# Block transposes on VectorE and SBUF transfers in place of TensorE transposes in the second block's attention

## The chip, the cores and the metric

The kernel runs on one core of a Trainium2 chip. The metric is device microseconds from start to end of one execution; the kernel before takes 1913.06 us (median of three runs, 1912.67 to 1913.16). Everything is float32; most matrix products run as three products of rounded parts (high by high, high by low, low by high), in the type fp32r.

## The reference, cut to what matters

Two blocks follow each other on a sequence of 512 positions with model width 2048. Only the second is touched: a projection to eight streams, eight heads of "stick-breaking" attention (A), eight heads of chunk-band attention (B), a gate, and an output projection.

```
h = rms_norm(x, norm_g)
qa, ka, va, ga, qb, kb, vb, gb = split(h @ w_in)
# A: w[t,s] = exp(log_sigmoid(z) + sum of log_sigmoid(-z) over s<j<t), s < t
ya = einsum('bhts,bhsd->bhtd', w, va)
# B: q, k normed per head, bias by distance, band of 9 chunks of 64
yb = einsum('bhcip,bhcpd->bhcid', softmax(scores + bias), vband)
x  = x + concat(ya * silu(ga), yb * silu(gb)) @ w_out
```

## The kernel before

Activations lie transposed: channels on the 128 partitions, the 512 positions along the row. A "unit" is one tile of 128 output channels of a projection: 16 contraction tiles `k`, three matmuls of 512 columns each, 48 matmuls in one PSUM bank (`gemm`). Head `h` of the second block has eight units `u + j` with `u = U_D2 + 8h`: qa, ka, va, ga, qb, kb, vb, gb. The weights of a unit come by one 1 MB transfer that SyncE (SP) issues, as soon as the unit two before it has been split; ScalarE copies its high part (`hi`), VectorE subtracts for its low part (`lo`), for unit `u + j + 2` behind unit `u + j`.

TensorE's own order is written out by hand in `d2_head`. Between tiles of the units it puts the attention of the same head: scores A (unit 3, after two tiles), scores B (unit 6, before its last two tiles), the value products A (unit 5, after two tiles) and B (after unit 7). Weights and probabilities come out of the scores with queries on the partitions, and the product needs keys there; values come with channels on the partitions and need positions there. So TensorE transposes: four 128x128 blocks of the values and ten of the weights, for A and again for B, 28 in a head. They go to PSUM (`pb`), from where ScalarE and VectorE make high and low parts (`VTH`, `VTL`; `WBH`, `WBL`; `PTH`, `PTL`). Each engine has its list, and semaphores join them; whatever stands behind a waiting instruction on its engine waits too. Heads 0 to 6 are a loop, head 7 is written out; in it the splitting of the output projection's operands (`operand_hi`, `operand_lo`) stands between the steps of B. Lines: 1480 is any matmul, 1483 a transpose, 398 and 829 the splitting of weights, 422 and 838 that of operands, 245 the weight transfer.

Of the kernel before, what the change touches and what calls it, by code (L numbers as in the profile page):

```python
# [12 lines left out]
P = 128  # L13
S = 512
D = 2048
KT = D // P
NB = S // P
# [26 lines left out]
TURN_AT = 11  # L44
# [42 lines left out]
def build(nc, w, w_ab, xT, memT, rows_in, consts, negatives, params, ws_t, bs_b, ln_rows, rel, x1_dram, rows_dram, outT):  # L87
    with ExitStack() as ctx:
# [61 lines left out]
        VTH, VTL = vtok_t[:, 0:S], vtok_t[:, S:2 * S]  # L150
        WBH, WBL, PTH, PTL = w_hi_t[:, 0:n], w_lo_t[:, 0:n], parts[:, 0:n], parts[:, n:2 * n]
# [61 lines left out]
        def v3(a):  # L213
# [3 lines left out]
        UP = [0, 512, 896, 1152]  # L217
        UN = [S - P * b for b in range(NB)]
# [4 lines left out]
            mem_in1 mem_in2 mem_in3 mem_in4 next_in m_ps wab_in wab ab_mm ab_sb row_sq diag x_ps x_r  # L223
            mixed
            dve_steps act_steps 
            ab_ps ab_exp ab_act ab_g ab_cum ab_e ab_gc
# [7 lines left out]
            a_vps a_vtok a_hi a_lo a_z a_l a_x a_w a_tp a_wh a_wl a_o  # L234
            g_y g_sig b_sq b_sql b_hi b_lo b_ss b_r b_n b_vps b_vh b_vtok b_bias b_sc b_add b_max b_exp b_p b_tp b_pt b_ptl b_o 
# [7 lines left out]
        def _(sp):  # L243
# [27 lines left out]
            with sp.Fori(1, U_END // 2 - 1) as i:  # L271
                for slot in range(2):

                    sp.wait_ge(sem["hi"], 8 * i + 4 * slot + 4)
                    sp.wait_ge(sem["lo"], 8 * i + 4 * slot + 4)
                    load(2 * i + 2 + slot, slot)
# [111 lines left out]
        def _(act):  # L388
# [115 lines left out]
            act.wait_ge(sem["ab_exp"], 1)  # L504
# [5 lines left out]
            act.wait_ge(sem["ab_gc"], 1)  # L510
            A(gate["egl"][:, :], gate["a"][:, :], ACT.Exp)
            A(gate["ekd"][:, :], gate["t"][:, :], ACT.Exp).then_inc(sem["ab_e"], 1)
# [229 lines left out]
            def d2_head(h, last=False):  # L742
                u = 8 * h + U_D2

                def next_hi(j):
                    hi(u + j + 2, (U_D2 + j) % 2)

# [18 lines left out]
                for b in range(NB):  # L766
                    act.wait_ge(sem["a_tp"], NB * h + b + 1)
                    A(WBH[:, UP[b]:UP[b] + UN[b]], pb[b][:, 0:UN[b]], ACT.Copy).then_inc(sem["a_wh"], 1)

                for j in range(2):  # L770
                    act.wait_ge(sem["evac"], u + (5 + j))
                    A(SQ[0:H, :], Y[0:H, :], ACT.Square)
                    A(E[0:H, :], Y[H:P, :], ACT.Square).then_inc(sem["b_sq"], 1)
                    next_hi(4 + j)

                    rsqrt(E, pb[5][:, :], -1.0 / P, "b_ss", 2 * h + j + 1, "b_r")
                    act.wait_ge(sem["b_n"], 2 * h + j + 1)
                    A([QH, KH][j], [QB, KBN][j], ACT.Copy).then_inc(sem["b_hi"], 1)
# [5 lines left out]
                act.wait_ge(sem["b_vps"], h + 1)  # L784
                A(VTH, pb[4][:, :], ACT.Copy).then_inc(sem["b_vh"], 1)
# [4 lines left out]
                for b in range(NB):  # L790
                    act.wait_ge(sem["b_tp"], NB * h + b + 1)
                    A(PTH[:, UP[b]:UP[b] + UN[b]], pb[b][:, 0:UN[b]], ACT.Copy).then_inc(sem["b_pt"], 1)
                if last:
                    act.wait_ge(sem["mixed"], M1 + 2 * DN - 1)
# [11 lines left out]
            with act.Fori(0, DN - 1) as h:  # L806
                st.enter(h, 2 * NB + 2 + 2 + 2)
                d2_head(h)
                st.leave(DN - 1)
            d2_head(DN - 1, True)  # L810
# [9 lines left out]
        def _(dve):  # L820
# [56 lines left out]
            V.tensor_tensor(ab, ab, par[:, C_LN:C_LN + KT].rearrange("p (k j) -> p k j", j=1).broadcast_to([P, KT, AB]), ALU.mult)                .then_inc(sem["wab"], 1)  # L877
# [17 lines left out]
            dve.wait_ge(sem["ab_mm"], 1)  # L895
            dve.wait_ge(sem["x_r"], 1)
            V.tensor_tensor(pair(SS, 0), pair(pb[0][:, :], 0), pair(XR, 0), ALU.mult)
            V.tensor_tensor(pair(SS, 1), turned(pb[0][:, :]), turned(XR), ALU.mult).then_inc(sem["ab_sb"], 1)
            lo(U_V + 3, 1)
            dve.wait_ge(sem["ab_ps"], 1)  # L900
# [7 lines left out]
            V.tensor_tensor(gv["t"], gv["a"], gv["g"], ALU.max).then_inc(sem["ab_exp"], 1)  # L908
# [4 lines left out]
            V.scalar_tensor_tensor(gv["g"], gv["a"], -1.0, a8, ALU.mult, ALU.mult).then_inc(sem["ab_g"], 1)  # L913
# [3 lines left out]
            dve.wait_ge(sem["ab_cum"], 1)  # L917
# [3 lines left out]
            V.tensor_tensor(gate["t"][:, :], gate["a"][:, :], gate["gc"][:, :], ALU.subtract).then_inc(sem["ab_gc"], 1)  # L921
            dve.wait_ge(sem["ab_e"], 1)
# [404 lines left out]
            def d2_head(h, last=False):  # L1327
# [17 lines left out]

                for j, dst in enumerate((QA, KA, VA)):
                    unit(u + j)
                    V.scalar_tensor_tensor(dst, bank[slot(j)][:, :], SCALE if j == 0 else 1.0, R12, ALU.mult, ALU.mult)\  # L1348
                        .then_inc(sem["evac"], 1)
                    next_lo(j)  # L1350
# [3 lines left out]
                dve.wait_ge(sem["a_vps"], h + 1)  # L1354
                st.then(V.tensor_copy(VTH, pb[4][:, :]))
                V.tensor_tensor(VTL, pb[4][:, :], VTH.bitcast(F32), ALU.subtract).then_inc(sem["a_vtok"], 1)
# [13 lines left out]
                for b in range(NB):  # L1370
                    t = slice(UP[b], UP[b] + UN[b])
                    dve.wait_ge(sem["a_wh"], NB * h + b + 1)
                    V.tensor_tensor(WBL[:, t], pb[b][:, 0:UN[b]], WBH[:, t].bitcast(F32), ALU.subtract).then_inc(sem["a_wl"], 1)
                gate_silu(2 * h + 1, SGA)
                for j in range(2):
# [5 lines left out]
                    V.tensor_tensor(SQH[H:P, :], SQ[0:H, :], FOLD.bitcast(F32), ALU.subtract).then_inc(sem["b_sql"], 1)  # L1381
                    next_lo(4 + j)
                    if j == 0:
# [22 lines left out]
                V.tensor_tensor(VBT, bank[slot(6)][:, :], R12, ALU.mult).then_inc(sem["evac"], 1)  # L1406
                next_lo(6)
                for c in range(NB):
# [3 lines left out]
                    V.tensor_scalar(pc, pc, small[:, 4 + c:5 + c], None, ALU.mult).then_inc(sem["b_p"], 1)  # L1412
                dve.wait_ge(sem["b_vh"], h + 1)
                V.tensor_tensor(VTL, pb[4][:, :], VTH.bitcast(F32), ALU.subtract).then_inc(sem["b_vtok"], 1)
# [3 lines left out]
                for b in range(NB):  # L1418
                    t = slice(UP[b], UP[b] + UN[b])
                    dve.wait_ge(sem["b_pt"], NB * h + b + 1)  # L1420
                    V.tensor_tensor(PTL[:, t], pb[b][:, 0:UN[b]], PTH[:, t].bitcast(F32), ALU.subtract).then_inc(sem["b_ptl"], 1)
                if last:
# [6 lines left out]
                gate_silu(2 * h + 2, SGB)  # L1429
                dve.wait_ge(sem["b_o"], h + 1)  # L1430
                out = (h + DN) * S
                out = big[:, bass.ds(out, S)] if not isinstance(out, int) else big[:, out:out + S]
                V.tensor_tensor(out, pb[4][:, :], SGB, ALU.mult).then_inc(sem["mixed"], 1)
                dve.wait_ge(sem["mixed"], 2 * h + (M1 + 2))
                if last:
# [8 lines left out]
            with dve.Fori(0, DN - 1) as h:  # L1444
                st.enter(h, 1 + 4 * NB + 1 + 1 + NB + 2 + 2)
                d2_head(h)
                st.leave(DN - 1)
            d2_head(DN - 1, True)
# [29 lines left out]
        def _(pe):  # L1478
# [79 lines left out]
            def ab_gemm():  # L1558

                pe.wait_ge(sem["wab"], 1)  # L1560
# [7 lines left out]
                ins.then_inc(sem["ab_mm"], 1)  # L1568
# [17 lines left out]
            pe.wait_ge(sem["ab_sb"], 1)  # L1586
            for c in range(NB):
                ins = tp(pb[0][:, c * P:(c + 1) * P], blk(SS, c))
            ins.then_inc(sem["ab_ps"], 1)
# [3 lines left out]
            pe.wait_ge(sem["ab_g"], 1)  # L1593
# [4 lines left out]
            mm(pb[0][:, n:2 * n], C["ones"], gate["g"][:, :]).then_inc(sem["ab_cum"], 1)  # L1598
# [218 lines left out]
            def d2_head(h):  # L1817
# [11 lines left out]
                def values(hi_part, low_part):  # L1829

                    for b in range(NB):
                        t, out = slice(UP[b], UP[b] + UN[b]), pb[4][:, b * P:S]
# [5 lines left out]
                d2(1)  # L1838
                d2(2)
                d2(3, 0, 2)  # L1840
                pe.wait_ge(sem["evac"], u + 3)
                for c in range(NB):
                    ins = tp(pb[4][:, c * P:(c + 1) * P], blk(VA, c))
                ins.then_inc(sem["a_vps"], 1)

# [4 lines left out]
                d2(4, 0, TURN_AT)  # L1850

                pe.wait_ge(sem["a_w"], NB * h + NB)
                for b in range(NB):
                    for c in range(b, NB):
                        ins = tp(pb[b][:, (c - b) * P:(c - b + 1) * P], WB[:, DO[c] + b * P:DO[c] + (b + 1) * P])
                    ins.then_inc(sem["a_tp"], 1)
                d2(4, TURN_AT)
                d2(5, 0, 2)
                pe.wait_ge(sem["a_wl"], NB * h + NB)
                pe.wait_ge(sem["a_vtok"], h + 1)  # L1860
                values(WBH, WBL).then_inc(sem["a_o"], 1)
                for j in range(2):
                    d2(5 + j, 0 if j else 2, 8)
                    pe.wait_ge(sem["b_sql"], 2 * h + j + 1)
                    mm(pb[5][:, :], sums[:, P:2 * P], SQH).then_inc(sem["b_ss"], 1)
                    d2(5 + j, 8, 14)
                    if j == 1:
# [114 lines left out]
```

## Time and profile before

| | |
|---|---|
| median of the runs | 1913.06 us |
| profiled execution, span from first to last instruction | 1910.9 us |
| outside that span, against the median | 2.2 us |
| TensorE busy | 1903.4 us, 100% of the span |
| VectorE, ScalarE, GpSimd busy | 61%, 43%, 6% |
| one head of the second block, from gate to gate | 98.2 us |

The profile gives the profiled execution's span; its own time outside the span is not listed apart, and the 2.2 us above is the difference to the median. A busy share of a matmul engine counts instructions that overlap, so it only says that something was in flight; the rate is read from starts, or from the chain of waits, whose pieces follow each other without overlap.

### The profile page before, as it was taken

How to read it: one execution, taken by the hardware profiler on the slowest of the kernel's cores; microseconds unless marked ns; L12 is line 12 of the kernel's file. 1: busy time of each engine (PE TensorE's matmuls, PEld its weight loads, DVE VectorE, ACT ScalarE, POOL GpSimd, SP SyncE). 2: the span in 40 equal slices, each digit the busy share in tenths (PEclk: the TensorE clock that was granted, in tenths of full speed). 3: DMA queues.
4: the chain of work that ended last, by engine and by line, in shares of the span. 5: the costliest groups of instructions: out<-in, count | busy, mean ns of one | idle time of the engine just before them, and what ended most of it. 6: DMA issues, size and time to landing. Idle time of an engine off the chain costs nothing.

```text
span 1910.9 us, 27480 instructions
## 1 busy us (share of the span) xinstructions
PE 1903.4 (100%) x9126; PEld 1586.7 (83%) x9126; DVE 1172.9 (61%) x2193; ACT 817.9 (43%) x1603; POOL 112.1 (6%) x172
## 2 busy tenths in 40 slices
PE   9999999999999999999999999999999999999999
PEld 7788888888888888888888888888888888888887
DVE  6565687778877775634556565656564646466333
ACT  5653444544445434423444343434343434344211
POOL 0100011001111010001000000000000000000010
PEclk9999999999999999999999999999999999999999
DMA  8722232223232223344332222222222222223341
GB/s 323 297 89 88 78 99 78 71 71 99 77 77 77 69 73 112 123 152 143 121 116 72 91 90 88 93 88 93 88 89 92 71 102 79 88 88 121 137 160 66
DMA packets 33817, 202.09 MB, mean 106 GB/s; under 512 B 4592, under 2 KB 4720, under 8 KB 13296
## 3 DMA queue, kind: packets, MB, share of 16 engines
q1 hardware_dynamic: 23904, 165.95, 24.2%
q0 software_dynamic: 9728, 35.49, 6.8%
q8 instruction: 26, 0.43, 0.1%
q10 hardware_dynamic: 144, 0.10, 0.0%
q14 instruction: 15, 0.12, 0.0%
HBM read 193.10 MB, written 8.42 MB: 105 GB/s over the span
## 4 chain that ended last, share of the span: by engine, by line
PE 95%; DVE 2%; DMA 1%; ACT 1%; issue 0%; SPq 0%; DVEq 0%; ACTq 0%
PE gemm L1480 82%; PE pb L1480 12%; PE pb L1483 2%; DMA raw<-in_w 1%; DVE w_lo L829 1%; DVE act_lo L838 0%; DMA scratch<-in_memT 0%; ACT w_hi L398 0%; DVE scratch L1039 0%; ACT act_lo L435 0%; DVE parts L849 0%; DVE scratch L937 0%; ACT scratch L406 0%; ACT scratch L407 0%; ACT scratch L405 0%
## 5 line engine op out<-in xcount | busy, mean ns | idle before, releaser
L1480 PE MATMUL gemm<-act_hi,w_hi 128*128 128x512 f32 x2304 | 921.0, 400 | 0.2 <-DVE act_lo L838 0.2
L1480 PE MATMUL gemm<-act_lo,w_hi 128*128 128x512 f32 x2320 | 902.8, 389 | 0.1
L1480 PE MATMUL gemm<-act_hi,w_lo 128*128 128x512 f32 x2304 | 899.8, 391 | 0.0
L398 ACT ACTIVATE w_hi<-raw 128x512 fp32r<-128x512 f32 x616 | 337.3, 619 | 406.7 <-PE gemm L1480 385.9
L1480 PEld LDWEIGHTS gemm<-act_hi,w_lo 128*128 128x128 f32 x2304 | 432.4, 188 | 93.3
L1480 PEld LDWEIGHTS gemm<-act_lo,w_hi 128*128 128x128 f32 x2320 | 436.7, 188 | 83.4 <-ACT w_hi L398 0.4
L1480 PEld LDWEIGHTS gemm<-act_hi,w_hi 128*128 128x128 f32 x2304 | 433.4, 188 | 82.2 <-issue 0.8
L829 DVE TENSOR_TENSOR w_lo<-raw,w_hi 128x512 fp32r<-128x512 f32 x624 | 400.1, 696 | 144.7 <-ACT w_hi L398 137.2
L1480 PEld LDWEIGHTS pb<-scratch 128*128 128x128 f32 x932 | 136.0, 192 | 26.3 <-DVE scratch L1200 5.9
L1480 PE MATMUL pb<-scratch 128*128 128x128 f32 (+3 forms) x932 | 141.4, 279 | 2.2 <-DVE scratch L844 1.7
L1348 DVE SCALAR_TENSOR_TENSOR scratch<-gemm,scratch 128x512 f32<-128x512 f32 x24 | 16.6, 692 | 150.1 <-PE gemm L1480 149.9
L405 ACT ACTIVATE scratch<-scratch 128x512 f32<-128x512 f32 x56 | 35.2, 628 | 87.0 <-DVE scratch L1040 43.7
L338 POOL TENSOR_TENSOR scratch<-scratch,cst 128x256 f32<-128x256 f32 x56 | 47.4, 853 | 416.3 <-DVE scratch L1091 243.4
L417 ACT ACTIVATE scratch<-pb,eps 128x512 f32<-128x512 f32 x41 | 28.3, 690 | 97.8 <-PE pb L1480 97.8
L1039 DVE SCALAR_TENSOR_TENSOR scratch<-scratch,par 128x511 f32<-128x511 f32 (+2 forms) x72 | 54.0, 750 | 9.8 <-DVE scratch L1037 2.5
L713 ACT ACTIVATE scratch<-big 128x512 f32 (+1 forms) x16 | 10.1, 632 | 108.7 <-DVE big L1287 108.7
L1287 DVE TENSOR_TENSOR big<-gemm,scratch 128x512 f32 (+1 forms) x16 | 11.0, 687 | 69.1 <-PE gemm L1480 69.1
L594 ACT ACTIVATE scratch<-pb 128x128 f32<-128x128 f32 x40 | 11.1, 278 | 91.3 <-PE pb L1480 90.9
L1483 PEld LDWEIGHTS pb<-cst,scratch 128*128 128x128 f32 x364 | 42.9, 140 | 7.1 <-DVE scratch L999 0.3
L1483 PE MATMUL pb<-cst,scratch 128*128 128x128 f32 x364 | 48.5, 272 | 0.0
L371 POOL DMA_DIRECT2D scratch<-in_rel x7 | 3.8, 538 | 657.6 <-DVE scratch L1402 657.6
L406 ACT ACTIVATE scratch<-scratch 128x512 f32<-128x512 f32 x56 | 35.4, 632 | 1.8
(296 smaller groups left out, 1614.8 us busy)
## 6 DMA issues: line engine op xcount, KB each, us to landing
raw<-in_w SPq DMA_DIRECT2D x154, 1024.0 KB, 4.8
scratch<-in_rows_in POOLq DMA_DIRECT2D x6, 1024.0 KB, 8.5
big<-in_xT POOLq DMA_DIRECT2D x4, 1024.0 KB, 11.4
scratch<-rows POOLq DMA_DIRECT2D x16, 256.0 KB, 6.5
scratch<-in_xT POOLq DMA_DIRECT2D x16, 256.0 KB, 2.9
x<-big POOLq DMA_DIRECT2D x16, 256.0 KB, 2.3
scratch<-x POOLq DMA_DIRECT2D x16, 256.0 KB, 4.0
outT<-scratch POOLq DMA_DIRECT2D x15, 256.0 KB, 3.8
```

Of the source, the lines that this page charges most:

```text
L338: nc.gpsimd.tensor_tensor(v3(blk(ML, NB * (k % 2), 2)), pair(AT, 0), C[f"level{k}"].rearrange("p (c t) -> p c t", c=1).broadcast_to([P, 2, ...
L398: A(w_hi[slot][:, c], raw[slot][:, c], ACT.Copy).then_inc(sem["hi"], 1)
L405: st.then(A(E, SS, ACT.Exp, scale=-1.0))
L406: st.then(A(E, E, ACT.Ln, bias=1.0))
L417: st.then(A(dst, src, ACT.Ln, bias=eps[:, 0:1], scale=scale))
L594: A(UI[:, 0:P], pb[2][:, 0:P], ACT.Copy).then_inc(sem["u_sb"], 1)
L829: V.tensor_tensor(w_lo[slot][:, c], raw[slot][:, c], w_hi[slot][:, c].bitcast(F32), ALU.subtract)\
L1039: st.then(V.scalar_tensor_tensor(Y[:, 3 - k:], SS[:, :S - 3 + k], tap(k), Y[:, 3 - k:], ALU.mult, ALU.add))
L1287: V.tensor_tensor(x1, bank[u0 % 2][:, :], blk(XIN, NB * j, NB), ALU.add).then_inc(sem["evac"], 1)
L1348: V.scalar_tensor_tensor(dst, bank[slot(j)][:, :], SCALE if j == 0 else 1.0, R12, ALU.mult, ALU.mult)\
L1480: return nc.tensor.matmul(out, a, b, start=start, stop=stop, skip_group_check=skip)
L1483: return nc.tensor.transpose(out, a, C["ident"])
```

## The change

In heads 0 to 6 no TensorE transpose is left; in head 7 only the ten of the probabilities B stay. VectorE transposes each 32x32 block within its rows' quadrant (`turn_values`, `turn_weights`) into `VTURN` or `SPB`, and SP issues 16 transfers (`regroup`) that move, for each pair of partition quadrants, 32 rows from the one into the other, into `VRAW` or `WB`. A row of one transfer has 512 bytes for values and 1280 for weights. ScalarE then copies the high part and VectorE subtracts the low part, both reading in one order and writing in another (`by_row`, `in_order`). The value products move: A from tile 2 to tile 12 of unit 5, B from the end of its head to tile 2 of the next head's unit 1 (in head 7 it stays behind unit 7). B's gate and its product with the output follow into the next head. Head 0 is written out as well, so the loop has heads 1 to 6. SP's list for the second block is written out, with waits for the turns between the weight loads. The renamed semaphores of the first block (`ab_*`) change no order.

```diff
+            def regroup(dst, src, size, done):
+                n = size * Q
+                for a in range(NB):
+                    for q in range(NB):
+                        sp.dma_start(dst[q * Q:(q + 1) * Q, a * n:(a + 1) * n], src[a * Q:(a + 1) * Q, q * n:(q + 1) * n])\
+                            .then_inc(sem[done], 16)
+            for h in range(DN):
+                u = U_D2 + 8 * h + 4
+                one_load(u)
+                one_load(u + 1)
+                sp.wait_ge(sem["v_turn"], 2 * h + 1)
+                regroup(VRAW, VTURN, NB, "va_in")
+                one_load(u + 2)
+                one_load(u + 3)
+                sp.wait_ge(sem["w_turn"], 2 * h + 1)
+                regroup(WB, SPB, SLOTS, "aw_in")
+                one_load(u + 4)
+                one_load(u + 5)
+                sp.wait_ge(sem["v_turn"], 2 * h + 2)
+                regroup(VRAW, VTURN, NB, "vb_in")
+                one_load(u + 6)
+                if h < DN - 1:
+                    sp.wait_ge(sem["w_turn"], 2 * h + 2)
+                    regroup(WB, SPB, SLOTS, "bp_in")
+                one_load(u + 7)
...
+            def value_hi(ready, n):
+                act.wait_ge(sem[ready], n)
+                A(in_order(VTH, NB), by_row(VRAW, NB), ACT.Copy).then_inc(sem["v_hi"], 1)
+            def weight_hi(ready, n):
+                act.wait_ge(sem[ready], n)
+                for s in (slice(0, SLOTS // 2), slice(SLOTS // 2, SLOTS)):
+                    A(in_order(WBH, SLOTS)[:, s], by_row(WB, SLOTS)[:, s], ACT.Copy).then_inc(sem["a_wh"], 1)
...
+                if tail:
+                    weight_hi("bp_in", 256 * h)
                 for j in range(3):
                     next_hi(j)
...
-                for b in range(NB):
-                    act.wait_ge(sem["a_tp"], NB * h + b + 1)
-                    A(WBH[:, UP[b]:UP[b] + UN[b]], pb[b][:, 0:UN[b]], ACT.Copy).then_inc(sem["a_wh"], 1)
+                value_hi("va_in", 256 * h + 256)
                 for j in range(2):
                     act.wait_ge(sem["evac"], u + (5 + j))
                     A(SQ[0:H, :], Y[0:H, :], ACT.Square)
                     A(E[0:H, :], Y[H:P, :], ACT.Square).then_inc(sem["b_sq"], 1)
+                    if j == 0:
+                        weight_hi("aw_in", 256 * h + 256)
                     next_hi(4 + j)
...
                 next_hi(6)
-                act.wait_ge(sem["b_vps"], h + 1)
-                A(VTH, pb[4][:, :], ACT.Copy).then_inc(sem["b_vh"], 1)
+                value_hi("vb_in", 256 * h + 256)
...
+            def turn_values(src):
+                V.transpose(by_row(VTURN, NB), src).then_inc(sem["v_turn"], 1)
+            def turn_weights(src, c):
+                n = min(c + 1, NB - 1)
+                ins = V.transpose(by_row(SPB, SLOTS)[:, c:c + 3 * n - 2:3], src[:, DO[c]:DO[c] + n * P])
+                if c == NB - 1:
+                    ins = V.transpose(by_row(SPB, SLOTS)[:, 7:8], src[:, DO[c] + n * P:DO[c] + DNN[c]])
+                return ins
...
+                if tail:
+                    gate_silu(2 * h, SGB)
+                    weight_lo(4 * h - 2)
...
+                for i, c in enumerate(reversed(range(NB))):
+                    dve.wait_ge(sem["a_w"], NB * h + i + 1)
+                    ins = turn_weights(WB, c)
+                ins.then_inc(sem["w_turn"], 1)
                 gate_silu(2 * h + 1, SGA)
+                value_lo(2 * h + 1, "a_vtok")
...
-                d2(1)
+                d2(1, 0, 2)
+                if tail:
+                    pe.wait_ge(sem["mixed"], 2 * h + (M1 - 1))
+                    pe.wait_ge(sem["b_vtok"], h)
+                    pe.wait_ge(sem["a_wl"], 4 * h)
+                    values(WBH, WBL, UT).then_inc(sem["b_o"], 1)
+                d2(1, 2)
```

## Rows read from the trace of the kernel before

**Rows 1.** The page: busy times, granted clock in 40 slices, and the chain's engines.

```profile
PE 1903.4 (100%) x9126; PEld 1586.7 (83%) x9126; DVE 1172.9 (61%) x2193; ACT 817.9 (43%) x1603; POOL 112.1 (6%) x172
...
PEclk9999999999999999999999999999999999999999
...
PE 95%; DVE 2%; DMA 1%; ACT 1%; issue 0%; SPq 0%; DVEq 0%; ACTq 0%
```

**Rows 2.** Busy time by stretch: stretch, length, busy (instructions) by engine, clock, DMA.

```profile
1289.40:1387.60 98.20, 98.20 (x462) 82.25 (x461) 57.11 (x108) 41.06 (x84) 0.54 (x1) 1.00 0.25 88
```

**Rows 3.** Chain of waits through that head: start, us, what, count.

```profile
1295.81 1.09 PE pb L1483 x10
1296.90 4.81 PE gemm L1480 x21
...
1303.57 4.14 PE gemm L1480 x18
...
1307.94 10.88 PE gemm L1480 x48
...
1329.03 0.44 PE pb L1483 x4
1329.47 4.13 PE gemm L1480 x18
1333.60 1.09 PE pb L1483 x10
1334.69 4.11 PE gemm L1480 x18
1338.80 1.85 PE pb L1480 x12
...
1374.73 0.44 PE pb L1483 x4
```

**Rows 4.** All transposes: duration min/median/max in ns, first and last start.

```profile
L1483 PE MATMUL pb<-cst,scratch x364: 270/272/328, 60.8 to 1727.3; 128*128 128x128 f32 x182
```

**Rows 5.** VectorE in order of time: start, us, instruction, idle before it.

```profile
1290.47 2.49 DVE L829 TENSOR_TENSOR w_lo<-raw,w_hi 128x512 fp32r<-128x512 f32 x4
...
1300.46 0.69 DVE L1377 TENSOR_TENSOR scratch<-gemm,scratch 128x512 f32<-128x512 f32 x1 [1.26 <-PE gemm L1480]
...
1327.14 0.68 DVE L1406 TENSOR_TENSOR scratch<-gemm,scratch 128x512 f32<-128x512 f32 x1
...
1332.62 0.49 DVE L1412 TENSOR_SCALAR scratch<-scratch,small 128x512 f32<-128x512 f32 x1
...
1338.84 0.69 DVE L1338 TENSOR_TENSOR scratch<-gemm,scratch 128x512 f32<-128x512 f32 x1 [2.45 <-PE gemm L1480]
...
1351.64 0.69 DVE L1348 SCALAR_TENSOR_TENSOR scratch<-gemm,scratch 128x512 f32<-128x512 f32 x1 [5.43 <-PE gemm L1480]
```

**Rows 6.** ScalarE in order of time: the four exponentials that finish weights A.

```profile
1290.53 1.53 ACT L764 ACTIVATE scratch<-scratch 128x512 f32<-128x512 f32 x4
```

**Rows 7.** The first block's block transposes on VectorE, durations in ns.

```profile
L1188 DVE STREAM_TRANSPOSE scratch<-scratch x40: 431/438/441, 258.1 to 696.4; 128x256 f32<-128x256 f32 x40
```

**Rows 8.** SP's issue instructions: duration min/median/max in ns, first and last start.

```profile
L245 SPq DMA_DIRECT2D raw<-in_w x154: 327/333/343, 11.1 to 1867.6; - x154
...
L249 SPq DMA_DIRECT2D raw<-in_w x6: 403/468/707, 1.0 to 5.2; - x6
```

**Rows 9.** DMA issues: KB each, median us from issue to landing.

```profile
outT<-scratch SPq DMA_DIRECT2D x1, 256.0 KB, 2.0
```

**Rows 10.** Head 7's end: VectorE, ScalarE (order of time), TensorE (chain).

```profile
1719.99 0.68 DVE L1406 TENSOR_TENSOR scratch<-gemm,scratch 128x512 f32<-128x512 f32 x1
...
1726.93 1.43 ACT L792 ACTIVATE parts<-pb 128x512 fp32r<-128x512 f32 x4 [1.36 <-PE pb L1483]
1728.21 4.29 ACT L422 ACTIVATE act_hi<-big 128x512 fp32r<-128x512 f32 x8
...
1733.51 174.16 PE gemm L1480 x768
```

More of the change, by code:

```diff
@@ L270, in _, with loads, one_load @@
                     mem(12, 4, "mem_in4")
[L271 to L276, printed above, removed]
+            def loads(first, past):
+                with sp.Fori(first // 2 - 1, past // 2 - 1) as i:
+                    for slot in range(2):
+                        sp.wait_ge(sem["hi"], 8 * i + 4 * slot + 4)
+                        sp.wait_ge(sem["lo"], 8 * i + 4 * slot + 4)
+                        load(2 * i + 2 + slot, slot)
+            def one_load(u):
+                sp.wait_ge(sem["hi"], 4 * (u - 1))
+                sp.wait_ge(sem["lo"], 4 * (u - 1))
+                load(u, u % 2)
+            def regroup(dst, src, size, done):
[4 more added lines that the diff above has]
+                            .then_inc(sem[done], 16)
+            loads(4, U_D2 + 4)
+            for h in range(DN):
[17 more added lines that the diff above has]
+                one_load(u + 7)
+            loads(U_O2 + 4, U_END)
             sp.wait_ge(sem["evac"], U_O2 + KT)
@@ L804, in d2_head @@
                 next_hi(7)
-            with act.Fori(0, DN - 1) as h:
-                st.enter(h, 2 * NB + 2 + 2 + 2)
+            d2_head(0, False)
+            with act.Fori(1, DN - 1) as h:
+                st.enter(h - 1, 2 * NB + 2 + 2 + 2)
                 d2_head(h)
-                st.leave(DN - 1)
-            d2_head(DN - 1, True)
+                st.leave(DN - 2)
+            d2_head(DN - 1, True, True)
             act.wait_ge(sem["mixed"], M1 + 2 * DN)
@@ L1353, in d2_head @@
                         V.tensor_tensor([QL, KL][j], dst, [QH, KH][j].bitcast(F32), ALU.subtract).then_inc(sem["a_lo"], 1)
-                dve.wait_ge(sem["a_vps"], h + 1)
-                st.then(V.tensor_copy(VTH, pb[4][:, :]))
-                V.tensor_tensor(VTL, pb[4][:, :], VTH.bitcast(F32), ALU.subtract).then_inc(sem["a_vtok"], 1)
+                    if j == 0 and tail:
+                        dve.wait_ge(sem["b_o"], h)
+                        out = (h + (DN - 1)) * S
+                        out = big[:, bass.ds(out, S)] if not isinstance(out, int) else big[:, out:out + S]
+                        V.tensor_tensor(out, pb[4][:, :], SGB, ALU.mult).then_inc(sem["mixed"], 1)
+                        dve.wait_ge(sem["mixed"], 2 * h + M1)
                 for i, c in enumerate(reversed(range(NB))):
@@ L1411, in d2_head @@
                     st.then(V.reciprocal(small[:, 4 + c:5 + c], small[:, 4 + c:5 + c]))
-                    V.tensor_scalar(pc, pc, small[:, 4 + c:5 + c], None, ALU.mult).then_inc(sem["b_p"], 1)
-                dve.wait_ge(sem["b_vh"], h + 1)
-                V.tensor_tensor(VTL, pb[4][:, :], VTH.bitcast(F32), ALU.subtract).then_inc(sem["b_vtok"], 1)
+                    if last:
+                        V.tensor_scalar(pc, pc, small[:, 4 + c:5 + c], None, ALU.mult).then_inc(sem["b_p"], 1)
+                    else:
+                        st.then(V.tensor_scalar(pc, pc, small[:, 4 + c:5 + c], None, ALU.mult))
+                        ins = turn_weights(PB, c)
+                if not last:
+                    ins.then_inc(sem["w_turn"], 1)
+                value_lo(2 * h + 2, "b_vtok")
                 if last:
@@ L1417, in d2_head @@
                         operand_lo(k, 4 * KT)
[L1418 to L1422, printed above, removed]
+                    for b in range(NB):
+                        t = slice(UP[b], UP[b] + UN[b])
+                        dve.wait_ge(sem["b_pt"], b + 1)
+                        V.tensor_tensor(PTL[:, t], pb[b][:, 0:UN[b]], PTH[:, t].bitcast(F32), ALU.subtract).then_inc(sem["b_ptl"], 1)
                     for k in range(4, 8):
@@ L1428, in d2_head @@
                         operand_lo(k, 4 * KT)
[L1429 to L1435, printed above, removed]
+                    gate_silu(2 * h + 2, SGB)
+                    dve.wait_ge(sem["b_o"], h + 1)
+                    V.tensor_tensor(big[:, (h + DN) * S:(h + DN + 1) * S], pb[4][:, :], SGB, ALU.mult).then_inc(sem["mixed"], 1)
+                    dve.wait_ge(sem["mixed"], 2 * h + (M1 + 2))
                     for k in range(12, KT - 1):
@@ L1442, in d2_head @@
                     next_lo(7)
[L1444 to L1445 removed]
+            d2_head(0, False)
+            with dve.Fori(1, DN - 1) as h:
+                st.enter(h - 1, 4 * NB + 1 + 1 + 2 * NB + 2 + 2)
                 d2_head(h)
[L1447 to L1448 removed]
+                st.leave(DN - 2)
+            d2_head(DN - 1, True, True)
             def out_tile(i, j, more=True):
@@ L1814, in _, with d2_head @@
             gemm(U_D2, U_D2 % 2, 12, KT, before=3 * KT)
-            def d2_head(h):
+            def d2_head(h, tail=True, last=False):
                 u = 8 * h + U_D2
@@ L1827, in scores, with values @@
                     return mm3(pb[c][:, 0:DNN[c]], (QH, QL), (KH, KL), c, slice(0, DNN[c]))
-                def values(hi_part, low_part):
+                def values(hi_part, low_part, at):
                     for b in range(NB):
-                        t, out = slice(UP[b], UP[b] + UN[b]), pb[4][:, b * P:S]
+                        t, out = slice(at[b], at[b] + UN[b]), pb[4][:, b * P:S]
                         mm(out, blk(VTH, b), hi_part[:, t], b == 0, False, skip=True)
@@ L1849, in d2_head @@
                 d2(3, 2)
[L1850 to L1861, printed above, removed]
+                d2(4)
                 for j in range(2):
-                    d2(5 + j, 0 if j else 2, 8)
+                    d2(5 + j, 0, 8)
                     pe.wait_ge(sem["b_sql"], 2 * h + j + 1)
                     mm(pb[5][:, :], sums[:, P:2 * P], SQH).then_inc(sem["b_ss"], 1)
-                    d2(5 + j, 8, 14)
-                    if j == 1:
+                    if j == 0:
+                        d2(5, 8, VALUES_AT)
+                        pe.wait_ge(sem["mixed"], 2 * h + M1)
+                        pe.wait_ge(sem["a_vtok"], h + 1)
+                        pe.wait_ge(sem["a_wl"], 4 * h + 2)
+                        values(WBH, WBL, UT).then_inc(sem["a_o"], 1)
+                        d2(5, VALUES_AT)
+                    else:
+                        d2(6, 8, 14)
                         pe.wait_ge(sem["b_lo"], 2 * h + 2)
@@ L1870, in d2_head @@
                             scores(c, QB, KBN).then_inc(sem["b_sc"], 1)
-                    d2(5 + j, 14)
-                d2(7, 0, 4)
-                pe.wait_ge(sem["evac"], u + 7)
-                pe.wait_ge(sem["mixed"], 2 * h + (M1 + 1))
-                for c in range(NB):
-                    ins = tp(pb[4][:, c * P:(c + 1) * P], blk(VBT, c))
-                ins.then_inc(sem["b_vps"], 1)
-                d2(7, 4, 10)
-                pe.wait_ge(sem["b_p"], NB * h + NB)
+                        d2(6, 14)
+                if not last:
+                    d2(7)
+                    return
+                d2(7, 0, 10)
+                pe.wait_ge(sem["b_p"], NB)
                 for b in range(NB):
```

101 lines of the change are left out of this document (60 added, 41 removed).

## The prediction

> **What bounds the kernel now.** I read the page first. TensorE is busy 100% of the span, the chain that ended last lies on it for 95%, and the granted clock is at its full step in every slice [rows 1], which is the 2.4 GHz level. The busy share alone would prove little, since matmuls overlap. So I took one head of the second block: in 98.20 us no idle time of TensorE, VectorE busy 57.11 and ScalarE 41.06 [rows 2]. The chain of waits through this head is TensorE alone, and its pieces add without overlap [rows 3]. A whole unit of 48 matmuls takes 10.88 us there, 0.2267 us a matmul. The bound is therefore the list of TensorE's instructions: what is taken from it shortens the time one for one, as long as no other engine becomes late.
>
> **What is removed.** In a head the chain holds 10 transposes at 1.09 us twice and 4 at 0.44 us twice, 3.06 us [rows 3]. The matmuls after them run a little long too: 21 in 4.81 against 21 x 0.2267 = 4.76, 18 in 4.13 and 18 in 4.11 against 4.08. That adds 0.05 + 0.05 + 0.03 = 0.13 (the value product has such a tail too, 18 in 4.14; it stays). Some of it may be a change of data type that the scores bring anyway, so a head gives 3.06 to 3.19; I take 3.13. Seven heads give 21.9. Head 7 keeps ten, and gives 0.44 + 0.44 + 1.09 + 0.1 = 2.1. Together **24.0 us** (23.4 to 24.4). The matmul instructions that stay keep their number; only their place changes, which costs nothing while TensorE does not wait.
>
> The row of all transposes shows 272 ns each [rows 4], yet ten together advance the chain by 1.09 us, 109 ns each, as the next starts while the last drains. The Trainium skill ("TensorE: Matmul & The Clock Gate", Part 4) gives about 275 ns for a transpose in a kernel; the duration agrees. By that price the 214 transposes would be worth 58.9 us and the time would be 1854. I go by the chain, because only it adds up to the span.
>
> **What VectorE and ScalarE get.** Per head VectorE turns values twice and weights twice. A block transpose of 256 columns takes 438 ns [rows 7]; with about 1 ns a column (a 512-column operation beside it takes 690, by [rows 5]), 512 columns take 0.7 and the five pieces of the weights about 1.9 us in sequence. That is 5.2 us a head, less one copy of 0.7: VectorE goes from 57 to about 62 of 95 us. ScalarE gets 0.6 more. Neither becomes the bound; what counts is when each result is there.
>
> **The new chain A: turn, 16 transfers, high part, low part, product.** In the old clock of the head in [rows 3, 5, 6]: the exponentials end at 1292.06 and VectorE's low part of the weights at 1292.96. Turns to 1294.9, SP starts at 1295.0. Let s be SP's time for one issue. The trace has no row of 16 issues of 32 rows. The nearest are the weight loads, issued singly, 0.333, and the pieces at the kernel's start, issued back to back, median 0.468 and up to 0.707 [rows 8]; the latter ran with other transfers still queued. Between them I take s = 0.43, and keep 0.33 and 0.7 as ends. The last transfer lands 2.0 us after its issue, as the 256 KB store does [rows 9]: 1295.0 + 15 x 0.43 + 2.0 = 1303.5. ScalarE's two copies of 640 columns and VectorE's two subtractions need 2.5 us more: 1306.0. TensorE arrives at tile 12 of unit 5 so: unit 5 begins 15 matmuls into the 21 behind the ten transposes, 1296.90 + 15 x 0.229 = 1300.3 [rows 3], less 1.14 for those transposes, plus twelve tiles of 0.68 and 0.23 for the sum, 1307.5; an instruction starts some 0.1 before its piece of the chain, 1307.4. Slack 1.4 us; it is gone at s = 0.52. Behind ScalarE's wait stand the high parts for unit 6, due five microseconds later, so this wait itself costs nothing.
>
> **Chain B.** The values leave PSUM at 1327.8 [rows 5], are turned at 1328.6, and 16 issues end at 1335.5. The probabilities were ready at 1333.1 [rows 5]; with 0.7 for the values' turn, 1.9 for their own and some waits, 1336.1. SP issues one weight load (0.33) and then 16 more: landed at 1336.2 + 6.45 + 2.0 = 1344.7, low parts at 1347.1. The product stands at tile 2 of the unit that followed the evacuation at 1351.64; 1.6 of transposes less, 0.35 that TensorE is ahead of that row, 1.36 of two tiles: 1351.0. Slack 3.9 us, gone at about s = 0.57.
>
> **SP's own list.** The load of unit 6 would have been issued 3.2 us behind unit 2; now it waits for the values' 16 issues, until about 8.5 us behind it, and lands in 4.8. It is split only behind unit 4, more than 20 us after unit 2. The other loads lose less. Cost: none; without this cover a late load would hold ScalarE, VectorE and TensorE in turn. GpSimd's queue is not touched.
>
> The Trainium skill ("DMA: Bandwidth & Descriptors", Rules for kernel authors) speaks against this change: transfers under 64 KB are mostly overhead, some 2 us each, and should be made one. These have 16 and 40 KB. By that rule the time would be rival 5's. The pieces at the kernel's start speak against that: they were issued about every half microsecond [rows 8], less than any landing time there [rows 9], so none waited for the one before to land.
>
> **Head 7's end.** Here there is no later unit to hide in. Values B leave PSUM at 1720.7 [rows 10], turned 1721.5, landed at 1721.7 + 15 x 0.43 + 2.0 = 1730.2; before, ScalarE had its copy at 1722.9. Behind the wait on ScalarE stand four operand copies and the copies of the probabilities. After the landing come 0.6 for the values, 2.2 for four operands (eight take 4.29) and 1.43 for the probabilities [rows 10], and VectorE's subtractions chase them; the last low part is there 5.2 us after the landing, at 1735.4. TensorE was ready when the projection's piece began less the product before it (1.85 [rows 3]), 1733.51 - 1.85 = 1731.6, now 0.5 earlier for the transposes gone, 1731.1. It stands **4.3 us** (3 at s = 0.33, 8 at 0.7). The operands after it keep some slack: the last one is due 10.2 us into the projection's first unit and comes about 1 us before.
>
> **Sum.** -24.0 + 4.3 = -19.7. On the profiled span, 1910.9 - 19.7 = 1891.2; with the 2.2 us that the median has outside that span, **1893.4 us**.
>
> **Rivals.**
> 1. *A small stall in every head* (s between 0.52 and 0.6, slower landing beside the 1 MB load, or longer turns with scattered output). At s = 0.6 A misses by 1.1 and B by 1.1: 8.8 + 7.7, and the end 6.9, so 1912.5; with A alone missing by half a microsecond, 1898. For it: A has only 1.4 us. Against: the single issues of 0.333. Time 1897 to 1911.
> 2. *SP's issue is the price, and it is slower than before.* One mechanism: 64 issues a head in one in-order list. It decides from s = 0.6 on. At 0.65 A misses by 1.8 us in eight heads and B by 2.7 in seven, 15 + 19, and the end costs 7.6: 1913 - 24 + 42 = 1931. For it: the row reaching 0.707. Against: those issues carried 128 rows and stood behind a full queue.
> 3. *The end hides its wait*: head 7 costs at most 1 us, 1890. For: the trace shows ScalarE idle there in places [rows 10]. Against: the order of ScalarE's list.
> 4. *A transpose costs its duration*: 214 x 0.272 [rows 4] less the end's 4.3, 1859. Against it, the pieces of the chain, which leave no room for it.
> 5. *The transfers run one after another*: 16 x 2.0 [rows 9] = 32 us for each regrouping instead of 8.5, over 20 us late in each of 15 products, above 2200. It is what the skill's rule on small transfers would make of them. Against it, the issues at the start.
>
> **Chances.** Forecast 0.60, rival 1 0.18, rival 2 0.08, rival 3 0.10, rivals 4 and 5 0.02 each. The range reaches from rival 3 into rival 1: 1889 to 1903. No change means within 0.2% (3.8 us), about what a measurement of this kernel can tell: it needs s near 0.6, chance 0.03 out of rival 1. Slower 0.10 (rivals 2 and 5), faster 0.87.
>
> **What would show it.** A head's period of 95.1 us in the chain, with no idle time of TensorE before either value product. SP's 16 issues every 0.43 us, about 6.9 us from first to last; landing about 2 us behind issue. One idle time of TensorE of about 4.3 us before the value product of head 7, put down to VectorE's last low part. The forecast fails if the heads show idle time before the products (rival 1 or 2, told apart by the issue rows), or if the span falls by more than 24.4.

## The result and the profile after: slower by 1.9%

The changed kernel takes 1949.69 us (median of 4, 1948.9 to 1950.7) beside 1913.11 for the kernel before: ratio 1.0194, 95% interval 1.0181 to 1.0206. The forecast was 1893.4, in a range of 1889 to 1903. Its span is 1948.3 us.

The page of the changed kernel first: busy time, share and instructions of each engine, and the chain's shares by engine.

```profile
PE 1898.6 (97%) x8912; PEld 1575.4 (81%) x8912; DVE 1201.2 (62%) x2246; ACT 818.8 (42%) x1581; POOL 112.2 (6%) x172
...
PE 70%; SPq 11%; DVE 11%; DMA 3%; ACT 3%; issue 2%; DVEq 0%; ACTq 0%
```

The 214 matmul instructions are gone (9126 before [rows 1]), but the chain that ended last, 95% TensorE before, now passes through SP's queue for 11% and VectorE for 11%. TensorE's waits say where (engine and line that waited, releaser: us in total, times, longest):

```profile
PE pb L1579 <- DVE w_lo_t L1406: 34.4, 15, 4.1
PE pb L1579 <- DVE parts L1523: 6.8, 1, 6.8
```

L1579 is any matmul, L1406 the low part of the turned weights. Product A and product B are the value products of the two attentions. Fifteen waits are the eight products A and the seven products B; the other is head 7's end. The profile names VectorE, but it only came last. Followed back from product A of head 0, the chain of waits shows what VectorE waited for (start, us, what):

```profile
1000.32 0.49 DVE scratch L1398
1000.81 0.19 DVE scratch L1400
1001.00 0.99 DVE scratch L1398 x3
1001.99 0.02 issue
1002.01 0.51 SPq L302
...
1011.66 0.59 SPq L302
1012.25 0.04 issue
1012.29 1.86 DMA scratch<-scratch
...
1014.18 0.75 ACT w_hi_t L798
...
1014.95 1.57 DVE w_lo_t L1406 x2
...
1016.66 1.47 PE pb L1579 x6
```

The turns take 1.7 us, the landing 1.86, the high and low parts 2.3, all close to the forecast. Between them SP (L302) issues 16 transfers, 0.59 us each with 0.04 between; the landing is counted from the start of the last issue. From the first issue to the last it is 10.3 us here, because one issue took 1.45 us, and 9.4 to 9.6 in the later batches of weights A. Product B, same columns, behind VectorE's row for the moment at which the values B leave PSUM:

```profile
1035.32 0.68 DVE L1501 TENSOR_TENSOR scratch<-gemm,scratch 128x512 f32<-128x512 f32 x1
...
1036.04 0.72 DVE scratch L1389
1036.78 0.51 SPq L302
...
1047.33 0.52 SPq L258
1047.85 0.04 issue
1047.90 0.51 SPq L302
...
1056.68 0.59 SPq L302
1057.27 0.04 issue
1057.31 1.87 DMA scratch<-scratch
...
1061.59 3.68 PE pb L1579 x12
```

This chain never leaves SP's list for 20 us: the values' 16 issues, a weight load, the probabilities' 16. VectorE had turned the probabilities by 1043.44; their first issue is at 1047.90, 4.5 us later. The last row shows something else: the product takes 3.68 us, where the kernel before needed 1.85 [rows 3]. The stretch around it, as busy time with the granted clock, says why:

```profile
1061.30:1065.50 4.20, 3.91 (x14) 3.58 (x15) 3.90 (x8) 1.87 (x4) 0.00 (x0) 0.59 0.22 94
```

The clock is 0.59 in the mean, so the lower level of 1.2 GHz for most of it (before, 1.00 in all of a head [rows 2]). It followed 4.1 us in which TensorE did nothing. The clock fell in six of the seven products B, which took 3.3 to 3.6 us by their starts in five cases and 2.65 in one. At the sixth, behind 3.7 us without work, it stayed at 1.00, and the product took 1.96 us.

```profile
1571.90:1576.10 4.20, 3.96 (x21) 3.50 (x22) 4.20 (x8) 1.82 (x4) 0.00 (x0) 1.00 0.21 90
```

All of SP's regrouping issues, and their landings:

```profile
L302 SPq DMA_DIRECT2D scratch<-scratch x496: 507/591/1575, 984.4 to 1759.0; - x166
...
scratch<-scratch SPq DMA_DIRECT2D x240, 40.0 KB, 1.9
...
scratch<-scratch SPq DMA_DIRECT2D x256, 16.0 KB, 1.8
```

The issues [rows 8] took 0.333 and 0.468. Head 7's end shows the chain that was forecast, with a longer issue part before it (left out between the two rows: ScalarE's copy of the values, 0.64 us, and VectorE's low parts of the values, 0.69, of four operands, 2.41, and of the probabilities, 1.60):

```profile
1758.99 1.81 DMA scratch<-scratch
...
1766.32 3.75 PE pb L1579 x12
```

From the landing to the product 5.5 us (5.2 forecast); TensorE stood 6.9.

**The balance.** Idle time of TensorE, each as the distance between two starts less a normal one: product A 9.4 us in eight heads (2.0 in the first, 1.0 to 1.2 in the others), product B 27.4 in seven (3.7 to 4.3), the end 6.9, together 43.7. The same kernel without any of these stalls measures 1889.75 (below). 1889.75 - 0.45 + 43.7 = 1933.0; up to 1949.7 there remain 16.7 us, which is not idle time. The head's period tells where most of it is. From one product A to the next it is 95.00 us without stalls; here it is 95.00 plus the stalls plus 1.8 us in four heads, 2.6 and 2.7 in two, and 0.3 in the one whose clock stayed up: 12.9 us together.

### The profile page after: what moved, and what is told of

Same layout as the page of the kernel before. It is cut to its first block, busy times and chain, and to the rows that moved or that the text cites. A ratio compares the mean times of both kernels' runs of the same rounds, so it can differ in the third digit from the quotient of the medians.

```text
span 1948.3 us, 27228 instructions
## 1 busy us (share of the span) xinstructions
PE 1898.6 (97%) x8912; PEld 1575.4 (81%) x8912; DVE 1201.2 (62%) x2246; ACT 818.8 (42%) x1581; POOL 112.2 (6%) x172
## 4 chain that ended last, share of the span: by engine, by line
PE 70%; SPq 11%; DVE 11%; DMA 3%; ACT 3%; issue 2%; DVEq 0%; ACTq 0%
PE gemm L1579 58%; SPq L302 11%; PE pb L1579 11%; DMA raw<-in_w 2%; DMA scratch<-scratch 2%; DVE w_lo L890 1%; DVE scratch L1457 1%; DVE w_lo_t L1406 1%; ACT w_hi L447 1%; DVE scratch L1458 1%; DVE small L1499 1%; PE pb L1582 1%; DVE scratch L1454 1%; DVE scratch L1497 1%; DVE scratch L1398 1%
## 5 line engine op out<-in xcount | busy, mean ns | idle before, releaser
L1579 PE MATMUL gemm<-act_hi,w_hi 128*128 128x512 f32 x2304 | 921.1, 400 | 0.2 <-DVE act_lo L899 0.2
L1579 PE MATMUL gemm<-act_lo,w_hi 128*128 128x512 f32 x2320 | 903.9, 390 | 0.4 <-DVE w_lo L890 0.4
L1579 PE MATMUL gemm<-act_hi,w_lo 128*128 128x512 f32 x2304 | 900.4, 391 | 0.0
L1579 PEld LDWEIGHTS gemm<-act_hi,w_lo 128*128 128x128 f32 x2304 | 433.0, 188 | 93.2
L1579 PEld LDWEIGHTS gemm<-act_lo,w_hi 128*128 128x128 f32 x2320 | 437.9, 189 | 84.9 <-ACT w_hi L447 0.7
L1579 PEld LDWEIGHTS gemm<-act_hi,w_hi 128*128 128x128 f32 x2304 | 434.8, 189 | 83.0 <-issue 0.8
L1579 PEld LDWEIGHTS pb<-scratch 128*128 128x128 f32 x932 | 136.4, 192 | 26.9 <-DVE scratch L1261 5.8
L1579 PE MATMUL pb<-scratch 128*128 128x128 f32 (+3 forms) x932 | 142.1, 280 | 2.2 <-DVE scratch L905 1.7
L1579 PE MATMUL pb<-w_hi_t,vtok_t 128*128 128x512 f32 (+3 forms) x120 | 37.5, 386 | 34.4 <-DVE w_lo_t L1406 34.4
L454 ACT ACTIVATE scratch<-scratch 128x512 f32<-128x512 f32 x56 | 35.2, 628 | 67.6 <-DVE scratch L1101 44.1
L1579 PEld LDWEIGHTS pb<-w_hi_t,vtok_t 128*128 128x128 f32 x120 | 26.8, 236 | 42.4 <-DVE w_lo_t L1406 33.0
L1406 DVE TENSOR_TENSOR w_lo_t<-scratch,w_hi_t 128x640 fp32r<-128x640 f32 x30 | 23.4, 821 | 54.1 <-ACT w_hi_t L798 54.1
L798 ACT ACTIVATE w_hi_t<-scratch 128x640 fp32r<-128x640 f32 x30 | 20.5, 729 | 69.8 <-DMA scratch<-scratch 69.8
```

What stands on the lines that cost most here:

```text
L454: st.then(A(E, SS, ACT.Exp, scale=-1.0))
L798: A(in_order(WBH, SLOTS)[:, s], by_row(WB, SLOTS)[:, s], ACT.Copy).then_inc(sem["a_wh"], 1)
L1406: V.tensor_tensor(in_order(WBL, SLOTS)[:, s], by_row(WB, SLOTS)[:, s], in_order(WBH, SLOTS)[:, s].bitcast(F32), ALU.subtract).then_inc(sem ...
L1579: return nc.tensor.matmul(out, a, b, start=start, stop=stop, skip_group_check=skip)
```

## The experiments

**What one issue costs.** Theory A: the price belongs to the form. Theory B: to the backlog of the queue.

```diff
             sp.wait_ge(sem["par_in"], 48)
...
+            for j in range(8):
+                sp.dma_start(VRAW[32 * (j % 4):32 * (j % 4) + 32, P * (j // 4):P * (j // 4) + P], VTURN[0:32, 0:P]).then_inc(sem["try_sp"], 16)
+            landed(8)
...
```

The other batches have the same shape, one for each form.

> The changed kernel with a tail added behind its last store: batches of 8 transfers from one queue, each form on a line of its own, so the span is some 60 us longer and only the issue rows count. In the heads SP's issues stand 0.633 us apart (0.59 each, landing 1.9). Theory A, the price belongs to the form (both ends in SBUF, constant addresses, 32 rows): SBUF to SBUF costs about 0.59 whether spaced by a wait for each landing or not, and forms with one end in HBM cost 0.40 to 0.45; the loop with a register address tells whether constants matter (0.33 if they do). Theory B, the price is the queue's backlog: the spaced batch costs 0.33 to 0.43 and batches of 1 MB-like loads cost more than 0.6. Same forms from ScalarE and GpSimd: 0.4 to 0.6 each by A, no view by B.

It took 2025.98 us in one run; only its issue rows count (min/median/max ns, start of first and last). In order: 32 rows of 512 B from SBUF to SBUF; 128 rows; 32 rows and 128 rows from HBM; 32 rows to HBM; 128 rows of 2 KB from HBM; 32 rows SBUF to SBUF with a wait for each landing; the same with 4 bytes a row, without the wait; a loop with a register address; ScalarE; GpSimd.

```profile
L335 SPq DMA_DIRECT2D scratch<-scratch x8: 570/591/592, 1947.0 to 1951.4; - x8
L338 SPq DMA_DIRECT2D scratch<-scratch x8: 565/602/602, 1953.2 to 1957.6; - x8
L341 SPq DMA_DIRECT2D scratch<-in_rel x8: 377/421/422, 1959.6 to 1962.8; - x8
L344 SPq DMA_DIRECT2D scratch<-in_rel x8: 363/432/433, 1964.4 to 1967.7; - x8
L347 SPq DMA_DIRECT2D x<-scratch x8: 338/422/429, 1969.8 to 1973.0; - x8
L350 SPq DMA_DIRECT2D big<-in_xT x8: 358/432/433, 1974.5 to 1977.7; - x8
L353 SPq DMA_DIRECT2D scratch<-scratch x8: 548/548/603, 1982.9 to 1995.5; - x8
L356 SPq DMA_DIRECT2D scratch<-scratch x8: 548/590/592, 1997.2 to 2001.6; - x8
L359 SPq DMA_DIRECT2D scratch<-scratch x8: 550/551/556, 2003.6 to 2010.2; - x8
L917 ACTq DMA_DIRECT2D scratch<-scratch x8: 604/612/682, 2017.6 to 2022.1; - x8
L469 POOL DMA_DIRECT2D scratch<-scratch x8: 496/496/517, 2012.5 to 2016.0; - x8
```

Theory A. With both ends in SBUF an issue costs 0.59 us, with one end in HBM 0.42, whichever end that is. Rows, bytes and the register address hardly matter (0.55 to 0.60). With an empty queue it still costs 0.548, so Theory B falls for this form: backlog adds 0.04. With one end in HBM it adds more: the first issue of each such batch took 0.34 to 0.38, the later ones 0.42 to 0.43, and in the heads the 1 MB load right behind sixteen issues took 0.52 (1047.33 above) where it takes 0.333 alone. Why the form with both ends in SBUF is the dearer one, no run shows.

**The same transfers, half as long a list.** GpSimd issues half of each batch, with semaphores of its own; ScalarE waits for both halves.

```diff
-                for a in range(NB):
+                for a in range(NB // 2):
                     for q in range(NB):
...
+                for a in range(NB // 2, NB):
+                    for q in range(NB):
+                        pool.dma_start(dst[q * Q:(q + 1) * Q, a * n:(a + 1) * n], src[a * Q:(a + 1) * Q, q * n:(q + 1) * n])\
+                            .then_inc(sem[done + "p"], 16)
...
```

> The 16 transfers of each regrouping are issued half by SP and half by GpSimd; same transfers, bytes and order of everything else. Theory 1 (the length of SP's issue list delays the value products): a batch takes 5.1 instead of 10.1 us, both products are ready in time, head period 95.1, the end stands 7.0 - 5.1 = 2 us: 1913.1 - 24.0 + 2.0 = 1891 us. Rival 2 (landing or traffic of the small transfers, or VectorE's turns, are late): unchanged at 1949 us. Rival 3 (GpSimd's issues cost as much as two of SP's): between, 1915 to 1949.

Measured 1891.70 us (1889.57 to 1895.04), ratio 0.9893 (0.9876 to 0.9909) to the kernel before, as in all runs below. The chain of waits of a head:

```profile
983.60 25.89 PE gemm L1598 x114
...
1012.43 1.85 PE pb L1598 x12
1014.29 8.22 PE gemm L1598 x36
...
1028.62 24.50 PE gemm L1598 x108
1053.12 1.85 PE pb L1598 x12
1054.98 21.82 PE gemm L1598 x96
```

It is TensorE alone again, both products take 1.85 us, and the heads follow each other every 95.00 us (95.1 forecast). SP needs 4.98 us for its eight issues and GpSimd 4.04 (probabilities B of head 0, start and us; the first row is the moment at which that head's values B leave PSUM):

```profile
1030.83 0.68 DVE L1520 TENSOR_TENSOR scratch<-gemm,scratch 128x512 f32<-128x512 f32 x1
...
1039.00 4.98 SPq L302 DMA_DIRECT2D scratch<-scratch  x8
...
1039.27 4.04 POOL L423 DMA_DIRECT2D scratch<-scratch  x8 [2.12 <-DVE scratch L1419]
```

Bytes, transfers and VectorE's turns are those of the changed kernel, so rival 2 of this run falls; rival 3 too. From the values B leaving PSUM, at 1031.5, to the start of product B's first matmul at 1053.0 it is 21.4 us; this is when TensorE gets there if nothing holds it, and it is needed below.

**The products later, the long list kept.**

```diff
-VALUES_AT = 12
+VALUES_AT = 15
...
-                d2(1, 0, 2)
+                d2(1, 0, 9)
...
-                d2(1, 2)
+                d2(1, 9)
```

> Only the places of the value products change: A at tile 15 instead of 12 of unit 5, B at tile 9 instead of 2 of the next head's unit 1. Theory 1 (fixed lateness of 1.95 us at A and 4.1 us at B, and half the clock behind the longer idle time): 2.0 and 4.8 us later suffice, no idle time in the heads, only the end remains with 7.0 us idle and 1.7 us of half clock: 1913.1 - 24.0 + 8.7 = 1898 us. Rival 4 (SP's list is a throughput limit, 64 x 0.633 us and the loads, so that lateness grows from head to head): a later place buys nothing, about 1949 us.

Measured 1906.49 us (1905.94 to 1908.59), ratio 0.997 (0.996 to 0.998). Nothing stands before the products, so the lateness was fixed, and rival 4 falls. But 8.5 us more than forecast remain, most of it in a wait that the changed kernel did not show (the second row):

```profile
PE pb L1579 <- DVE parts L1523: 6.7, 1, 6.7
PE pb L1579 <- DVE parts L1489: 5.5, 8, 0.7
```

L1489 is the low part of the normed keys B; TensorE loses about 0.86 us before the scores B of each head, 6.9 us of the 8.5; the other 1.6 are not accounted for. The changed kernel does not show this wait; there TensorE arrives 1.0 us or more later because of product A's stall, enough to cover 0.86.

**Later, and head 7's values by TensorE.** In addition to the edit above, head 7 takes the old way for the values B.

```diff
...
-                d2(7, 0, 10)
+                d2(7, 0, 4)
+                pe.wait_ge(sem["evac"], u + 7)
+                pe.wait_ge(sem["mixed"], 2 * h + (M1 + 1))
+                for c in range(NB):
+                    ins = tp(pb[4][:, c * P:(c + 1) * P], blk(VBT, c))
+                ins.then_inc(sem["b_vps"], 1)
+                d2(7, 4, 10)
```

> As the run before it with later places, and in head 7 the values B are turned by TensorE as in the kernel before. Theory 1: the end's 8.7 us go, 0.45 us of four transposes come back: 1913.1 - 23.6 = 1889.5 us. Rival 5 (the end stands for another reason, such as the operand copies in their new places): stays near 1898 us.

Measured 1898.33 us (1897.39 to 1899.74), ratio 0.9925 (0.9908 to 0.9941): 8.2 less than without it, as expected, with the same wait before the scores B left over.

**Split issue, head 7's values by TensorE.** Product places as in the changed kernel; both edits are those shown above, the second for head 7 alone.

```diff
+                for a in range(NB // 2, NB):
...
+                for c in range(NB):
+                    ins = tp(pb[4][:, c * P:(c + 1) * P], blk(VBT, c))
...
```

> The split issue of the run before (half SP, half GpSimd), and in head 7 the values B turned by TensorE. Theory 1: that run's end, 2.1 us idle and about 0.8 us of half clock, goes; four transposes (0.45) come back: 1891.7 - 2.5 = 1889.2 us. Rival 5 (something else holds the end): 1891.7 us.

Measured 1889.75 us (1888.52 to 1890.62), ratio 0.9875 (0.9859 to 0.9891). No wait of TensorE is left in the second block's heads. It beats both kernels; its lead over the split alone is 2 us, which the intervals do not tell apart.

**Both edits together.** The kernel of the last run, with the late products besides.

```diff
-VALUES_AT = 12
+VALUES_AT = 15
...
-                d2(1, 0, 2)
+                d2(1, 0, 9)
...
-                d2(1, 2)
+                d2(1, 9)
```

> Both at once: split issue, later places of the products (tile 15 of unit 5, tile 9 of the next unit 1), head 7's values B by TensorE. In the run with later places alone, 1.1 us stands before the scores B in each head, behind VectorE's low part of the normed keys. Theory 6: that wait comes from ScalarE standing for the weights' transfers in front of the high parts and the norms, so with short batches it is gone: 1889.2 us as with the split alone. Rival 7: it comes from the later place of product A itself: 8 x 0.9 more, 1896 us.

Measured 1889.95 us (1889.27 to 1890.22), ratio 0.9878 (0.9861 to 0.9894). Short batches with the late products: the wait before the scores B is gone, so it came from the long batch and not from the late place (rival 7 falls). The way is seen in the run with later places alone, in head 1, where product A starts at 1112.62:

```profile
1109.27 1.37 ACT L798 ACTIVATE w_hi_t<-scratch 128x640 fp32r<-128x640 f32 x2 [4.88 <-DMA scratch<-scratch]
...
1110.04 1.56 DVE L1406 TENSOR_TENSOR w_lo_t<-scratch,w_hi_t 128x640 fp32r<-128x640 f32 x2 [3.62 <-ACT w_hi_t L798]
```

ScalarE stands 4.9 us for the transfers and VectorE 3.6 us for ScalarE, both in front of the work that the scores B need; VectorE takes the keys B out of PSUM 3.9 us after product A began, and 2.8 us after it with short batches. The prediction had called ScalarE's wait free.

**Filling the idle time.** To see the clock apart from the stall:

```diff
+                    for _ in range(16):
+                        mm(pb[5][:, :], sums[:, P:2 * P], act_hi[:, 0:S])
                     pe.wait_ge(sem["mixed"], 2 * h + (M1 - 1))
                     pe.wait_ge(sem["b_vtok"], h)
                     pe.wait_ge(sem["a_wl"], 4 * h)
```

> The changed kernel with 16 extra matmuls of 512 columns, whose result nobody reads, in front of product B's wait: 3.63 us of work in an idle time of 3.7 to 4.5 us, in seven heads. Theory 8 (TensorE drops to its lower clock behind the long idle time, and the products then run at half rate): they fill idle time only and keep the clock; values of 3.5 us become 1.9: 1949.7 - 7 x 1.7 = 1938 us. Rival 9 (the slow products have another cause, their operands or traffic): no gain, 1949.7 us or some more.

Measured 1939.24 us (1935.64 to 1939.71), ratio 1.013 (1.0113 to 1.0147): 10.4 us faster than the changed kernel with 112 matmuls more. The stretch of the product now:

```profile
1060.00:1064.20 4.20, 3.97 (x22) 3.43 (x22) 4.20 (x8) 1.88 (x4) 0.00 (x0) 1.00 0.27 107
```

The clock stays at 1.00. So most of the 12.9 us behind the products B was the lower level: 10.4 came back, although the waits before product A grew by 1.4 us in these heads. Head 7's end has the lower level too: its product took 3.55 instead of 1.86, and four matmuls behind it 0.43 instead of 0.23, 2.5 us by the starts. Some of the rest is no matter of the clock: a product behind a stall took about 0.1 us more also at 1.00 (1.94 to 1.98, each product A). Of the 16.7 us, 12.9 and 2.5 are placed; 1.3 stay open, 0.6 of them the difference between the medians and the profiled executions.

**Only the values B from GpSimd.**

```diff
-                sp.wait_ge(sem["v_turn"], 2 * h + 2)
-                regroup(VRAW, VTURN, NB, "vb_in")
...
+                pool.wait_ge(sem["v_turn"], 2 * h + 2)
+                for a in range(NB):
+                    for q in range(NB):
+                        pool.dma_start(VRAW[q * Q:(q + 1) * Q, a * P:(a + 1) * P], VTURN[a * Q:(a + 1) * Q, q * P:(q + 1) * P])\
+                            .then_inc(sem["vb_in"], 16)
```

> Only the values B are issued by GpSimd (16 issues of about 0.54), all else stays with SP. Theory 1 says that product B is late because the probabilities' 16 issues stand behind the values' 16 on SP: they now start at once, 4.4 us earlier, so product B's idle time and its half clock go; product A keeps 1.2 us in each of eight heads, the end keeps 5.6 + 1.7: 1889.2 + 9.6 + 6.9 = 1906 us. Rival 10 (product B is late for its own batch's length or landing): product B keeps most of its 4 us, about 1945 us.

Measured 1908.45 us (1907.32 to 1911.81), ratio 0.9977 (0.9966 to 0.9987).

```profile
PE pb L1583 <- DVE w_lo_t L1410: 7.6, 8, 1.4
PE pb L1583 <- DVE parts L1527: 5.4, 1, 5.4
```

Eight waits instead of fifteen: product B's is gone although its own batch of 16 stayed with SP. It was late for what stood before it in the list. Rival 10 falls. Product A keeps its stall, 1.0 to 1.1 us by the starts and 1.6 in the first head.

## Why the prediction was wrong

- *The bound and what is removed*: right. 24.0 us were forecast and 0.45 come back with head 7's four transposes; 1913.27 (the kernel before, beside this run) - 1889.75 = 23.5 was measured, and a head takes 95.00 us. The transposes were worth 109 ns and not their duration; rival 4 falls.
- *Turns, landing, high and low parts*: right within 0.3 us each.
- *"Between them I take s = 0.43"*: the step that failed. The term was 0.633 from start to start (0.59 and 0.04). The limit in the same paragraph, s = 0.52 for product A, was good: with 0.633 in place of 0.43, A comes 15 x 0.2 = 3.0 us later and overdraws its slack of 1.4 by 1.6 (1.0 to 1.2 measured, and 2.0 in the first head, where one issue took 1.45); the end stands 4.3 + 3.0 = 7.3 (6.9). Both nearest rows had one end in HBM, the new transfers none. I had kept 0.7 as a bound, yet gave what lies beyond 0.6 only 0.08 and cut the range at 1903: the range did not take in the bound that I had named.
- *"Slack 3.9 us, gone at about s = 0.57"* (product B): wrong as well. The row at 1351.64 stands behind product B of the kernel before, 1.85 us of TensorE [rows 3]. The change takes this product out of that place, and the sum never took its 1.85 off. The slack was 2.1 us, gone at about s = 0.51. The split run confirms it: TensorE is there 21.4 us after the values B leave PSUM, and the forecast had 1351.0 - 1327.8 = 23.2. With s = 0.633, B comes 31 x 0.2 = 6.3 us later, less 0.3 that SP had waited, and overdraws 2.1 by 3.9; 3.9 in the mean was measured. At s = 0.43 the smaller slack would still have held, so the miss hangs on s; but 7 x 1.85 = 13 of product B's 27.4 us come from this slip.
- *Rival 2* is what happened, by its mechanism and its place: one in-order list with 64 issues a head. At s = 0.65 it said 1931, with 42 us of stalls; 43.7 were measured. That these two agree is luck: A was to cost 15 (9.4 measured), B 19 (27.4) and the end 7.6 (6.9), and the errors nearly cancel.
- *No term for the clock*: 16.7 us lie outside the stalls, most of them the lower level behind some 4 us of idle TensorE (10.4 came back when that time was filled). The trace before had no such idle time in the heads, so no row priced it; but the rivals stood on idle times of that length, and only the time while TensorE waits was counted.
- *"This wait itself costs nothing"* (ScalarE's for the weights): true at the forecast length. At the real one it costs 0.86 us a head in front of the scores B, seen once product A no longer stalled before it.
- *SP's own list*: right, the weight loads were late for nobody. *Rival 5*: wrong, the transfers overlap; landing 1.9 us after issue, with the next 0.63 behind. The Trainium skill ("DMA: Bandwidth & Descriptors", Anatomy of one DMA — SWDGE (gpsimd) path) gives a fixed cost of about 2.0 us per DMA, fitted on transfers that GpSimd issues. The landing of SP's transfers here, 1.9 us, agrees with it, but it was paid once for 16; what was paid 16 times is the issue.

## What to carry to other kernels

When work is traded for many small transfers, price the issuing queue first: number of issues times the time of one, for exactly that form, against the time until the consumer. If that form is in no trace and the point of decision lies between the bounds, both sides belong in the range. When a step changes its place, take its own time off the arrival of what used to stand behind it. Count an idle time of the saturated engine with what the lower clock takes afterwards, and look what stands behind each new wait once the stall that hid it is gone.

## What the runs showed of the hardware

- In a batch, a transfer's issue from SP took 0.59 us with both ends in SBUF (32 or 128 rows, 4 or 512 bytes a row) and 0.42 to 0.43 with one end in HBM (32 or 128 rows of 512 bytes, 128 rows of 2 KB). Single 1 MB loads took 0.333, and 0.52 right behind sixteen regrouping issues. GpSimd took 0.50 and ScalarE 0.61 for the SBUF form.
- Behind 3.7 to 4.3 us of idle time the granted clock fell to the lower level in six cases of seven, in an otherwise saturated kernel, and the twelve matmuls of a product took 3.3 to 3.6 us by their starts (2.65 in one case) instead of 1.86; in the seventh they took 1.96 at full clock. 16 matmuls without use, in the idle time, kept the clock up in all seven. Behind product A's 1.0 to 2.0 us it did not fall; behind 2.1 us at the end of the split run it did, and that product took 2.6 us.
- With half the issues on GpSimd, 40 KB transfers landed after 3.8 us (SP's) and 3.7 us (GpSimd's) instead of 1.9. The issues of a batch took 5 us less, and its last landing came about 7.5 us after the first issue instead of 11.3.
